# A short entry behind the width test of every mixture-of-experts pass, with the programs ahead of the loop

## The reference, cut to what matters

```python
def _moe_swiglu(h, w_router, w_gate, w_up, w_down):
    ...
    logits = (tok @ w_router).astype(jnp.float32)
    top_val, top_idx = lax.top_k(logits, TOP_K)
    weights = jax.nn.softmax(top_val, axis=-1)
    ...
    g = lax.ragged_dot(xs, w_gate, group_sizes)
    u = lax.ragged_dot(xs, w_up, group_sizes)
    y = lax.ragged_dot(jax.nn.silu(g) * u, w_down, group_sizes)
    y = y * weights.reshape(-1)[order][:, None].astype(y.dtype)
```

## Time and profile before

| | us |
|---|---|
| median of 3 runs | 3782.71 (3781.17 to 3785.42) |
| the profiled execution, its own time | 3778.69 |
| its span, first to last instruction | 3776.9 |
| TensorE matmul busy | 3555.7 (94%) |
| VectorE, ScalarE, GpSimd busy | 2236.9, 1661.8, 440.1 |
| mean granted TensorE clock, share of full speed | 0.971 |

### The profile page before, as it was taken

How to read it: one execution, slowest core, us unless ns; L and a number is a source line. 1 busy time by engine, 2 the same in 40 slices (tenths; PEclk the granted TensorE clock), 3 DMA queues, 4 the chain that set the end, 5 groups by cost and what they waited for, 6 DMA issues and landing times. The chain is left out here.

```text
span 3776.9 us, 60053 instructions
## 1 busy us (share of the span) xinstructions
PE 3555.7 (94%) x22342; PEld 3263.3 (86%) x22343; DVE 2236.9 (59%) x2845; ACT 1661.8 (44%) x1941; POOL 440.1 (12%) x365
## 2 busy tenths in 40 slices
PE   7999999999999976999999999989999999999997
PEld 4986577888888765899899999988999999999997
DVE  3558734445445556766555555568555675665776
ACT  5227543223232255755533344356443565444444
POOL 0007400000000001010000010001100000100673
PEclk8999999999999987999999999999999999999998
DMA  6604325223432126955444444469444575553763
GB/s 223 229 27 168 128 93 202 95 87 100 152 100 92 72 107 215 327 201 198 155 156 136 134 136 149 133 197 353 135 150 141 182 247 174 179 165 118 248 214 134
DMA packets 409793, 609.14 MB, mean 161 GB/s; under 512 B 23571, under 2 KB 337555, under 8 KB 409608
## 3 DMA queue, kind: packets, MB, share of 16 engines
q1 hardware_dynamic: 386152, 542.02, 42.3%
q0 software_dynamic: 23168, 63.86, 5.4%
q10 hardware_dynamic: 288, 1.05, 0.1%
HBM read 586.80 MB, written 41.98 MB: 166 GB/s over the span
## 5 line engine op out<-in xcount | busy, mean ns | idle before, releaser
L2698 DVE TENSOR_TENSOR moe_gu_lo<-moe_raw_gu_lo,moe_gu_hi 128x2048 fp32r<-128x2048 f32 x254 | 587.6, 2313 | 103.2 <-ACT moe_gu_hi L2517 102.8
L2517 ACT ACTIVATE moe_gu_hi<-moe_raw_gu_lo 128x2048 fp32r<-128x2048 f32 x254 | 485.8, 1913 | 254.0 <-DMA moe_raw_gu_lo<-in_moe_w_gate 193.6
L2321 PE MATMUL moe_g<-moe_x,moe_gu_hi 128*128 128x336 f32 (+3 forms) x1120 | 351.7, 314 | 20.2 <-issue 15.8
L2323 PE MATMUL moe_g<-moe_x,moe_gu_lo 128*128 128x336 f32 (+3 forms) x1120 | 351.4, 314 | 0.0
L2322 PE MATMUL moe_g<-moe_x,moe_gu_hi 128*128 128x336 f32 (+3 forms) x1120 | 350.8, 313 | 0.0
L2321 PE MATMUL moe_y<-moe_h,moe_d_hi 128*128 128x336 f32 (+3 forms) x1120 | 347.9, 311 | 0.2 <-DVE moe_y_t L2760 0.2
L2323 PE MATMUL moe_u<-moe_x,moe_gu_lo 128*128 128x336 f32 (+3 forms) x1120 | 346.9, 310 | 0.0
L2323 PE MATMUL moe_y<-moe_h,moe_d_lo 128*128 128x336 f32 (+3 forms) x1120 | 346.9, 310 | 0.0
L2321 PE MATMUL moe_u<-moe_x,moe_gu_hi 128*128 128x336 f32 (+3 forms) x1120 | 346.1, 309 | 0.0
L2322 PE MATMUL moe_y<-moe_h,moe_d_hi 128*128 128x336 f32 (+3 forms) x1120 | 346.0, 309 | 0.0
L2322 PE MATMUL moe_u<-moe_x,moe_gu_hi 128*128 128x336 f32 (+3 forms) x1120 | 346.0, 309 | 0.0
(11 more groups left out here) (445 smaller groups left out, 9333.6 us busy)
## 6 DMA issues: line engine op xcount, KB each, us to landing
moe_raw_gu_lo<-in_moe_w_gate SPq DMA_DIRECT2D x127, 1024.0 KB
moe_raw_gu_lo<-in_moe_w_up SPq DMA_DIRECT2D x127, 1024.0 KB
moe_raw_d_lo<-in_moe_w_down SPq DMA_DIRECT2D x126, 1024.0 KB
ffn_raw_d_lo<-in_ffn_w_down SPq DMA_DIRECT2D x22, 1024.0 KB, 4.8
proj_w_mod<-in_w_ada POOLq DMA_DIRECT2D x10, 2048.0 KB, 9.4
att_w_mod<-in_w_ada SPq DMA_DIRECT2D x10, 2048.0 KB, 7.6
ffn_first_raw<-in_ffn_w_gate SPq DMA_DIRECT2D x11, 1024.0 KB, 5.2
ffn_first_raw<-in_ffn_w_up SPq DMA_DIRECT2D x11, 1024.0 KB, 7.7
```

The lines of the kernel that those rows point to most:

```text
L2321: pe.matmul(bank[:, 0:width], wh, moving[:, 0, 0:width], start=start, stop=False)
L2323: return pe.matmul(bank[:, 0:width], wl, moving[:, 0, 0:width], start=False, stop=stop)
L2517: act.activation(hi[par][:, :, :], raw[par][:, :, :], ACT.Copy).then_inc(rounded, 1)
L2698: dve.tensor_tensor(lo[par][:, :, :], raw[par][:, :, :], hi[par][:, :, :].bitcast(F), ALU.subtract).then_inc(split, 1)
```

## The change

Each program is cut in two. The first part, `begin`, is placed in an **entry** directly behind the tree (in order of width, 25 of them), and ends with a hinted jump to the rest, the **program**. The 25 programs are now placed ahead of `tail`. What `begin` holds:

- TensorE: the wait for `x_split` and, of chunk 0, the 24 products of the first gate piece in a wide pass, the 32 matmuls of the first gate and up pieces in a narrow one, the 24 of the gate side in a few pass. The rest of chunk 0 stands in the program.
- ScalarE: the semaphore step or, in a few pass, the wait and the load of the gate row; then `round_g` of chunk 1.
- VectorE: the semaphore step, then `rest_g` of chunk 1, in a narrow pass too, where it stood behind `add_gate` before.

Inside the entry the hint is the first instruction. The first jump to `head` is hinted as well (`entered`). On ScalarE and VectorE the hint for the jump to `tail` moves from ahead of `ready_tokens` and the last additions to behind `load_width`, three tiles of result before the jump, and the few programs get one. ScalarE's `round_g` moves from the start of a step to the end of the step before, which leaves its order as it was. In the dense layer, which has no tests, `begin` and the program follow each other directly.

```diff
-        def each_width(eng, who, body):
+        def each_width(eng, who, begin, body, entered):
...
-            nc.br(head, engines=this)
+            eng.br(head).branch_hint(entered)
+            for k, width in enumerate(WIDTHS):
+                with nc.body(program(k + 1), valid_engines=this):
+                    leaving = body(this_pass(), width, 2 * width <= TOKENS, load_width)
+                    eng.br(tail).branch_hint(leaving)
             with nc.body(tail, valid_engines=this):
...
+                tree(1, len(WIDTHS), width_no)
+                for k, width in enumerate(WIDTHS):
+                    with nc.body(node(k + 1, k + 1), valid_engines=this):
+                        entering = eng.mark_branch_hint_location()
+                        begin(this_pass(), width, 2 * width <= TOKENS)
+                        eng.br(program(k + 1)).branch_hint(entering)
                 with nc.body(f"{end}_far", valid_engines=this):
                     eng.br(end)
-                for k, width in enumerate(WIDTHS):
-                    with nc.body(node(k + 1, k + 1), valid_engines=this):
-                        leaving = body(p, width, 2 * width <= TOKENS, load_width)
...
+            def begin_pass(p, width, narrow):
+
+                pe.wait_ge(x_split, (p + 1) * KD + 2)
+                if few(width):
+                    hidden_few(p, 0, parity(p, 0), (0,))
+                else:
+                    hidden(p, 0, parity(p, 0), width, narrow, range(begun(narrow)))
...
+            def begin_pass(p, width, narrow):
+                if narrow and not few(width):
+
+                    dve.sem_inc(y_added, (C - 1) * KD)
+                elif table is not None:
+
+                    dve.sem_inc(halves_added, 2 * C * FB)
+                rest_g(p, 1, parity(p, 1))
...
-                leaving = dve.mark_branch_hint_location() if table is not None else None
...
                 load_width(p + 1)
+                leaving = dve.mark_branch_hint_location() if table is not None else None
                 tiles = -(-width // P)
```

More of the change, by code:

```diff
@@ L2089, in node, with program, this_pass, tree @@
                 return f"{name}_{who}_widths_{first}_{last}"
-            def tree(first, last):
+            def program(k):
+                return f"{name}_{who}_program_{k}"
+            def this_pass():
+                return nc.snap(counter, min_val=0, max_val=passes)
+            def tree(first, last, width_no):
                 if first == last:
@@ L2102, in tree @@
                         eng.br(node(last, last))
-                tree(first, middle)
-                tree(middle + 1, last)
+                tree(first, middle, width_no)
+                tree(middle + 1, last, width_no)
             def load_width(p):
@@ L2407, in turn_result, with hidden_few @@
                         last.then_inc(y_turned, KD - (2 * tiles - 1) if final else 1)
-            def hidden_few(p, c, par):
+            def hidden_few(p, c, par, sides=(0, 1)):
                 n = p * C + c
-                early = type(c) is int and c < 2
-                if early and c == 0:
-                    pe.wait_ge(x_split, (p + 1) * KD + 2)
-                if not early:
+                if not (type(c) is int and c < 2):
                     pe.wait_ge(h_whole, (n - 1) * FB + H0)
-                for side, split in enumerate((g_split, u_split)):
-                    pe.wait_ge(split, n + W0 + 1)
+                for side in sides:
+                    pe.wait_ge((g_split, u_split)[side], n + W0 + 1)
                     bank = g_ps[par][:, side * CHUNK_FF:(side + 1) * CHUNK_FF]
@@ L2478, in one_pass @@
                     return pass_of_few(p, load_width)
-                hidden(p, 0, parity(p, 0), width, narrow)
+                hidden(p, 0, parity(p, 0), width, narrow, range(begun(narrow), 2 * FB))
                 def step(c, par):
@@ L2498, in one_pass @@
                 return leaving
+            entered = pe.mark_branch_hint_location() if table is not None else None
             if early is None:
@@ L2615, in step @@
                     round_d(p, c, par)
+                    if gate_after:
+                        round_g(p, c + 2, par)
                 def pooled_squares(tiles):
@@ L2649, in one_pass @@
                 load_width(p + 1)
+                leaving = act.mark_branch_hint_location() if table is not None else None
                 tiles = -(-width // P)
@@ L2660, in one_pass @@
                 return leaving
+            entered = act.mark_branch_hint_location() if table is not None else None
             if table is None:
@@ L2902, in one_pass @@
                 return leaving
+            entered = dve.mark_branch_hint_location() if table is not None else None
             if table is not None:
```

89 lines of the change are left out of this document (43 added, 46 removed).

## The result

| | before | after |
|---|---|---|
| median of the runs taken together, us | 3781.94 (3779.57 to 3785.42) | 3794.44 (3792.13 to 3802.05) |
| ratio after / before, 95% interval | | 1.0039 [1.0029, 1.0048] |
| the profiled execution, its own time | 3778.69 | 3793.61 |
| its span | 3776.9 | 3791.8 |

The account below looks back on a forecast made before the run. TensorE's waits for code ahead of passes 3, 4, 8 and 9 (15.2 us) were the prize, none won. Losses of 3.3 (wide), 2.3, 2.7, 2.3, 2.7 (passes 1, 2, 5, 7) sum to 13.3: 3782.7 to 3796 us, range 3773 to 3803.

Parts of the forecast that it names:

- The entry is not loaded when the tree jumps to it: TensorE, wide passes 3, 4, 8, 9: jumps miss as before; gain 0, loss 0.3 us in pass 8, 0.5 in 9.
- The second jump: TensorE, entry to program in wide passes: a miss partly covered, costing 0.8, 0, 0.5 and 1.2 us in passes 3, 4, 8, 9.
- What a hint does: All three engines: a hint only replaces what the next packet crossing asks for, so one shortly ahead of its jump is mostly dead.
- ScalarE and VectorE: Pass ends: the jump to `tail` misses (2.7 to 3.1 us), first work 2 us later where one jump missed before; wide passes absorb it.
- Pass 1: ScalarE comes 3 to 5 us later if hint `entered` is dead, with 1.7 to spare: 2.3 us lost, between 0 and 3.3.
- Pass 2: Narrow: the reordering loses 0.7 us at TensorE's chunk 1 remainder, 2.7 with ScalarE 2 us later.
- Pass 5: Few pass: ScalarE and VectorE two us later, straight onto TensorE's 4.38 us wait: 2.3 us lost, between 0 and 3.
- Pass 7: Narrow: ScalarE 1.4 us later and the reordered chain adds 1.3: 2.7 us lost, between 0 and 4.
- Pass 6, pass 8 and the end: Pass 6 and loop end: 0; pass 8: 0.3 us at the entry's jump and 0.5 at the second jump.
- hints at once: Rival, chance 0.15: hints fetch immediately, TensorE's second jump costs nothing, ScalarE and VectorE come earlier; -6 us, 3777.
- entries held: Rival, chance 0.10: wide entries are loaded when the tree jumps, saving the four exposed jumps; -15 to -20 us, 3765.
- Losses absorbed: Rival, chance 0.23: hints dead, but few and narrow passes catch up and the second jump is covered; 0 to 7 us, 3786.

Follow-up runs that it names:

- entry_chunk0: The changed kernel with all of chunk 0 in TensorE's entries, between hint and jump: 3797.7 us, 1.0038 against the kernel before.
- pe_only: TensorE's code as changed, ScalarE's and VectorE's as in the kernel before: 3789.2 us, ratio 1.0017 against the kernel before.
- moved_hints: The kernel before with ScalarE's and VectorE's hint for `tail` moved behind `load_width`, and one added in few programs: 3781.5 us, ratio 1.0000.
- act_dve_only: ScalarE's and VectorE's code as changed, TensorE's as in the kernel before: 3789.4 us, ratio 1.0025 against the kernel before.
- reorder_only: The kernel before with VectorE making chunk 1's remainder ahead of the first addition of halves in narrow passes: 3788.4 us, ratio 1.0013.
- no_entry_hint: The changed kernel without the hint at the head of every entry, on all three engines: 3794.7 us, ratio 1.0040 against the kernel before.
- look_ahead: The kernel before, with TensorE testing the next width and hinting its program ahead of the result's transposes, then jumping: 3771.9 us, ratio 0.9971.
- before_no_hints: The kernel before with every hint taken away on all three engines: 3793.0 us, ratio 1.0033 against the kernel before.

## Why the prediction was right, point by point

The forecast was 3796 us, the median is 3794.4, and the forecast's mechanism, entries held no better than programs and hints dead in them, is what the trace shows. The sum of 13.3 us against 12.5 is better than its terms were, by luck: errors of both signs met in it. (The upper bounds listed there add up to 18.3 us and not 19, which would end the range at 3801 and not 3803.)

- **The entry is not loaded when the tree jumps to it**: right, 3.5 to 4.0 us in passes 3, 4, 8 and 9. Pass 7 I had not listed: the jump into its program took 0.42 us before, the jump into its entry takes 2.0, and the wait ahead of its first product grows from 1.17 to 2.83 us. The four waits of the wide passes grew by 1.4 us in all (15.8 to 17.2), where I had 0.8. How many packets a hint or the move into a packet brings, no run shows; in its place stand the tree's jumps themselves, 3.36 to 4.01 us into the five wide entries.
- **The second jump**: missed in all eight passes, as forecast. The cover was mis-sized twice. For wide passes I forecast 0.8, 0, 0.5 and 1.2 us of bubble; it is 0 in all four. I took the sequencer's row behind the 24 products, 3.0 us after the first product, for the moment when it reaches the jump; it reaches it 1.6 us after the first product (3492.2 against 3490.53), so 4 us of products are queued, not 2.5. And for few and narrow passes I had no term at all, where 24 or 32 short products cover less: 2.33 us in pass 5 and 1.43 in pass 7. The first step failed to the high side by 2.5 us, the second to the low side by about 4; TensorE's part alone measured +6.4 us, and I had 3.3. The cover in wide passes is itself a gift of the first miss: at the full clock of pass 9 (32 products in 4 us) its 24 products would last 3.0 us, of which by this estimate 1.4 would be left when the jump is reached, against a miss of 3.7.
- **What a hint does**: "a hint only replaces what the next crossing asks for" fits TensorE's packets in `entry_chunk0` and `pe_only` (two between hint and jump where it took 0.31 to 0.43 and 1.05 us, at most one where it took 3.3 to 4.0 in the changed kernel), but it stays a reading. One inference under it fails: in the kernel before, a packet starts between the hint and the jump to `tail` in only two of nine passes (3 and 9), so in the others the short jump is no sign of a fetch.
- **ScalarE and VectorE**: I forecast a gap of 2.5 us or more behind the jump to `tail` in nearly every pass. VectorE has it behind all but the two few passes. ScalarE has it in passes 1, 2 and 5, 1.2 us behind pass 9 and 0.4 or less behind the other five, where the jump hit. `moved_hints` shows that the hint's new place is not the reason by itself, so the layout has a part in it; what it is stays open. The 1.2 us in place of 3.5 behind the last pass fit the 1.5 us that come back there, where I had 0: `act_dve_only` has 1.1 us of gap and gets 1.2 back.
- **Pass 1**: 2.3 forecast; the wait in chunk 0 grew from 2.35 to 3.54 us and later chunks lost some more: 2.9 from its first product to that of pass 2.
- **Pass 2**: 2.7 forecast, 3.7 measured in the same way (6.6 for both passes, against 6.2 above, since pass 1 starts 0.5 us earlier after). The reordering was the mis-sized term: 0.7 forecast, 2.2 by itself in `reorder_only`. I had let `round_u` start as soon as silu was done and TensorE take the remainder with 0.1 us to spare; the whole chain moved by the length of `rest_g`.
- **Pass 5**: 2.3 forecast. Passes 4 and 5 lost 6.4 by the two first profiles, of which 2.6 is the wait that comes and goes. The remaining 3.8 is TensorE's own second jump more than the other engines (`act_dve_only` loses 2.5 us in pass 5, hardly more than the 2.2 of the second profile of before; `pe_only` loses 5.2): the wait of 4.38 us shrank to 2.34, since TensorE had already lost its time 6 us earlier. So the step "two us more, straight onto the 4.38" failed; the loss came from another place and was partly absorbed there.
- **Pass 7**: 2.7 forecast, 0 measured from start to start. The two waits are gone, and 1.43 us of issue, with a start 1.7 us later, stand in for them. The reordering, after which the pass took 3.1 us longer in `reorder_only` (1.2 in the second profile of before), hides behind TensorE's own lateness: the other two engines' part alone loses 2.6 us there, both parts together nothing.
- **Pass 6, pass 8 and the end**: 0 forecast for pass 6 and the end; +1.8, most of it pass 7's start, and -1.5. Pass 8 lost 1.9, of which 0.7 is the longer wait ahead of pass 9.

The rival "hints at once" falls with `no_entry_hint`, and "entries held" with the tree's jumps. "Losses absorbed" was right for wide second jumps and for pass 7, but not for the sum. The sum came out since the missing term (few and narrow second jumps) and the mis-sized reordering were about as large as the bubbles and the pass 7 term that did not come.

## What to carry to other kernels

In this kernel a prefetch hint was worth what stood between it and its jump. What went with it was not the number of instructions as such but the packets: with entries of 24 or 32 matmuls at most one packet of TensorE's code started between the two, the same as without the hint, and the jump took 3.3 to 4.0 us; with entries of 64 or 96 there were two, and it took 0.31 to 0.43. In the look ahead six of eight jumps took 0.32 to 0.43. Where the jump came too early, 2.3 to 2.7 us passed from the start of the last packet ahead of it to its end. So decide the jump early and put real work of common code between hint and jump, rather than cut a short entry that must itself be fetched. Count the misses on every path before cutting code in two: the second jump's 3.3 to 4.0 us were hidden in the wide passes, where the work queued ahead lasted some 4 us, and left 2.33 us of idle time in the few pass 5 and 1.43 in the narrow pass 7.

## What the runs showed of the hardware

- A hint by itself started no packet in pass 5 of `look_ahead`: none started within 2.4 us of the hint, and one started 0.5 to 0.8 us after the next jump was through. In `entry_chunk0` the jump of the hint that did nothing in the changed kernel took 0.31 to 0.43 us in seven of eight passes, each with two packets between hint and jump. Pass 2 of `pe_only` also had two, and its jump took 1.05 us; with one it took 3.87 us in the changed kernel. What starts the fetch, and why a second packet started in that entry of `pe_only`, I could not settle. For ScalarE and VectorE, which share a queue (q14), the packets don't say whose they are.
- On TensorE the unhinted jumps into programs and entries that missed in full took 3.2 to 4.3 us (3.25 and 4.34 in `before_no_hints`), six hinted jumps of `look_ahead` 0.32 to 0.43 us. Of the nine jumps to `tail` in `before_no_hints` seven took 0.17 to 0.31 us with no hint. In six of these `tail` had run before, and 4 to 7 packets of TensorE's code had started since; for the two that missed (3.37 and 3.85 us) it was eight.
- An exposed miss cost more than its wait. Behind 3.2 to 4.9 us of idle time TensorE ran the next 4 us at a granted clock of 0.50 (passes 3, 4 and 9 of before and after, pass 8 of after), behind the 2.90 us of pass 8 of before at 0.58. Where `look_ahead` took a miss away, that gave back the wait and, in pass 3, 1.9 us more.
- Two profiles of the same code differed by 6.3 us in span, 3.1 of it ahead of the changed part and 2.6 in a single wait. With effects of 5 to 12 us a second profile of before is worth its time.
